# A block of 48 unused floats ahead of the normed activations in SBUF

## The reference

```
x = x + concat([y_a, y_b]) @ ev_w_out            # after h @ ev_w_in
x = x + conv_glu_ffn(rmsnorm(x), w_up, ..., w_down)
qkv = rmsnorm(x) @ od_w_qkv ;  x = x + y @ od_w_out
h = rms_norm(x) * (1 + scale) + shift            # second block
x = x + g * ((silu(h @ w_gate) * (h @ w_up)) @ w_down)
```

## Time and profile before

| | |
|---|---|
| median of three runs | 1253.51 us (1252.48 to 1256.44) |
| profiled execution: span | 1253.0 us |
| TensorE matmul busy | 1230.9 us, 98% of the span, 9987 matmuls |
| TensorE weight load busy | 1147.4 us, 92% |
| VectorE busy | 933.6 us, 75% |
| ScalarE busy | 703.9 us, 56% |
| TensorE on the chain that ended last | 97% of the span |
| granted TensorE clock | 0.999 of full |
| read from HBM | 261.17 MB, 209 GB/s |

### The profile page before, as it was taken

One profiled execution on the slowest core, in us unless ns is written; L12 is line 12 of the kernel. 1 busy time (PEld: TensorE's weight loads), 2 busy tenths in 40 slices (PEclk: granted clock), 3 DMA queues, 4 the chain that ended last, 5 costly groups with the idle time before them and its releaser, 6 DMA issues.

```text
span 1253.0 us, 23639 instructions
## 1 busy us (share of the span) xinstructions
PE 1230.9 (98%) x9987; PEld 1147.4 (92%) x9987; DVE 933.6 (75%) x1260; ACT 703.9 (56%) x1032; POOL 20.1 (2%) x31
## 2 busy tenths in 40 slices
PE   6999999999999999999999999999999999999998
PEld 6999889999999879999988998999998998999997
DVE  5888369888758777999987566899976666677453
ACT  6843477555555767666657556634445554643432
POOL 0002000000000000000000000000000000000000
PEclk9999999999999999999999999999999999999999
DMA  9450277776567256689653534899965356675540
GB/s 322 168 201 4 69 247 246 250 238 229 193 220 257 105 170 234 217 291 319 249 201 119 194 130 148 290 360 351 343 234 202 136 204 200 236 250 188 202 169 34
DMA packets 163683, 263.78 MB, mean 211 GB/s; under 512 B 5677, under 2 KB 98041, under 8 KB 163578
## 3 DMA queue, kind: packets, MB, share of 16 engines
q1 hardware_dynamic: 160586, 259.54, 60.3%
q10 hardware_dynamic: 2992, 2.72, 0.7%
HBM read 261.17 MB, written 1.05 MB: 209 GB/s over the span
## 4 chain that ended last, share of the span: by engine, by line
PE 97%; DVE 1%; ACT 1%; DMA 1%; issue 1%; SPq 0%; DVEq 0%; ACTq 0%
PE ps L1109 26%; PE ps L1080 17%; PE ps L1082 16%; PE ps L1081 16%; PE ps L847 2%; PE ps L848 2%; PE ps L849 2%; PE ps L1095 2%; PE ps L1097 2%; PE ps L1096 2%; PE ps L2397 2%; PE ps L827 1%; DMA ring<-in_ev_w_in_dram 1%; PE ps L2406 1%; PE ps L2597 1%
## 5 line engine op out<-in xcount | busy, mean ns | idle before, releaser
L623 DVE TENSOR_TENSOR wlo<-ring,whi 128x2048 fp32r<-128x2048 f32 x194 | 443.3, 2289 | 97.6 <-ACT whi L617 97.6
L1080 PE MATMUL ps<-ghi,whi 128*128 128x256 f32 x1600 | 449.0, 281 | 0.0
L1081 PE MATMUL ps<-glo,whi 128*128 128x256 f32 x1600 | 446.8, 279 | 0.0
L1082 PE MATMUL ps<-ghi,wlo 128*128 128x256 f32 x1600 | 446.5, 279 | 0.0
L617 ACT ACTIVATE whi<-ring 128x2048 fp32r<-128x2048 f32 x194 | 370.4, 1913 | 96.7 <-PE ps L1109 69.7
L1080 PEld LDWEIGHTS ps<-ghi,whi 128*128 128x128 f32 x1600 | 300.4, 188 | 2.0 <-DVE wlo L623 0.6
L1081 PEld LDWEIGHTS ps<-glo,whi 128*128 128x128 f32 x1600 | 299.7, 187 | 0.8
L1082 PEld LDWEIGHTS ps<-ghi,wlo 128*128 128x128 f32 x1600 | 300.4, 188 | 0.0
L1109 PE MATMUL ps<-whi,yhi 128*128 128x512 f32 x480 | 159.7, 396 | 0.7 <-DVE ylo L1996 0.7
L1109 PE MATMUL ps<-wlo,yhi 128*128 128x512 f32 x480 | 156.7, 390 | 0.0
L1109 PE MATMUL ps<-whi,ylo 128*128 128x512 f32 x480 | 156.6, 390 | 0.0
(11 more groups left out here) (314 smaller groups left out, 1575.0 us busy)
## 6 DMA issues: line engine op xcount, KB each, us to landing
arena<-in_w_ada_dram SPq DMA_DIRECT2D x48, 1024.0 KB, 6.0
ring<-in_ff_w_up_dram SPq DMA_DIRECT2D x44, 1024.0 KB, 7.6
ring<-in_w_gate_up_dram SPq DMA_DIRECT2D x44, 1024.0 KB, 7.5
ring<-in_ff_w_down_dram SPq DMA_DIRECT2D x10, 2048.0 KB, 7.9
ring<-in_w_down_dram SPq DMA_DIRECT2D x10, 2048.0 KB, 7.8
ring<-in_od_w_qkv_dram SPq DMA_DIRECT2D x6, 2048.0 KB, 8.6
ring<-in_w_qkv_dram SPq DMA_DIRECT2D x6, 2048.0 KB, 7.9
ring<-in_w_in_dram SPq DMA_DIRECT2D x6, 2048.0 KB, 8.1
```

The costliest lines, as they stand in the source:

```text
L623: e.tensor_tensor(shaped(WLO[i % NB], k), v, shaped(WHI[i % NB], k).bitcast(F32), ALU.subtract).then_inc(S["w_lo"], 1)
L1080: e.matmul(o, wh, h[0][:, k, :], start=k == 0, stop=False)
L1081: e.matmul(o, wh, h[1][:, k, :], start=False, stop=False)
L1082: x = e.matmul(o, wl, h[0][:, k, :], start=False, stop=k == NK - 1)
```

## The change

One line is added behind the declaration of `adahi` and `adalo`. It declares a block of 48 floats (192 bytes per partition) which nothing reads or writes:

```diff
         AHI, ALO = (sb(f"ada{i}", 512, F32R)[:, :] for i in ("hi", "lo"))
+        sb("gap_h", 48)
         MIX, PRE, SOLVE = ExitStack(), ExitStack(), ExitStack()
         RW = part(MIX, "mix", 32 * 256)
         HT0 = [c3(part(PRE, f"h{i}", NK * T, F32R)[:, :], NK) for i in ("hi", "lo")]
```

## The result

The changed kernel takes 1270.13 us in the median (1269.39 to 1270.59), the kernel before 1254.88 us in the same comparison. The ratio is 1.0129, 95% interval 1.0117 to 1.0141. The forecast was no change, so it was wrong. The profiled execution has a span of 1268.7 us, 15.7 more than before.

A forecast was written before the change was run, and what follows sets the result against it. TensorE, busy 1230.9 of 1253.0 us, was taken as the bound, the change acting only through matmul pace. All terms were 0 us, so the forecast was the median, 1253.5 us, range 1230 to 1261, no change at 0.52.

The forecast's parts named there:

- The four readings: Four observations from the profile, claiming that a tile's start doesn't decide between the paces of 113.3 and 117.7 ns.
- Reading 1: `pe_tile`, moving input at 960, stationary at 128 or 640: the same addresses give both paces, 113.3 and 117.7 ns.
- Reading 2: `pe_rows`, weights moving from 128, activations stationary from 960 or 448: the same two paces as `pe_tile`, 113.3 and 117.7 ns.
- Reading 3: Line 1109, both inputs already placed as after the change: 226.9 ns for 512 columns, so nothing below 113.3 ns gained.
- Reading 4: Weight loads on lines 1080, 1109 and 1096: 188 or 189 ns whether read from 128 or from 960 or 448.
- rows 4, 5 and 7: Profile timeline stretches of `pe_tile` (4, 5) and `pe_rows` (7), at 113.3 and 117.7 ns; cited for 0 us pace change.
- rows 9: Profile rows of weight loads, 188 or 189 ns at all offsets shown; cited for 0 on the 1248 matmuls with stationary activations.
- The upper bound: Most the tile matmuls could lose: 1680 on `pe_rows`, `pe_first` and `hhi` by 4.4 ns, 7.4 us.
- quick stretches turning slow: Rival: stretches at 113.3 ns (quick) go to 117.7 (slow), 3.7 to 7.4 us more, 1257 to 1261 us; chance 0.09.
- the collision: Rival: load and moving input, at the same offset, collide; 6480 matmuls by 4.4 ns, 28.5 us, 1262 to 1282 us; chance 0.09.
- The tiles turning quick: Rival: slow tile matmuls go to 113.3 ns, 21.1 us less; nearly all, 1230 to 1235 us, 0.15; part, 1236 to 1249, 0.13.
- The rule: The skill's step of N / 2.4 + 2.5 ns, 109.2 for 256 columns; reaching it would save 44 us, 1209 us; chance 0.02.

The follow-up runs named there:

- the sweeps: Separate kernels of matmul streams alone, weights at 128 or 960, sixteen activation starts 64 bytes apart: at distance 0 120.0 ns, at 64 and 192 113.3 or 117.8.

## Why the prediction was wrong

**What bounds the kernel** held: TensorE's pace is all of the change, and the scratch tiles behind `glo` cost nothing when they alone moved (1254.39 us against 1253.51 in the same comparison).

**The four readings** were right as rows and wrong as an argument. *Reading 1*: the same addresses give both paces. True, and it shows that a start doesn't fix the pace; it doesn't show that another start can't bring other paces. *Reading 2*: swapping the inputs changes nothing. By the sweeps the distances of the two kinds are 64 and 192, mirror images, and both have the pair 113.3 and 117.8. The swap that I took for a test of the offset was a test of its sign. *Reading 3* was true as written: line 1109, at distance 0, has 113.4 ns for each 256 columns, so both inputs at 128 "buy nothing below 113.3 ns". But it was the only row with both inputs at 128, and I let it stand for the short matmul. For 512 columns 0 is a good distance (227 against 232 at 128), for 256 columns it settles at the slowest pace seen (120.0). What the long matmul shows doesn't hold for the short one. *Reading 4*: loads take 188 ns at all offsets. It had no row of a 256-column matmul at distance 0, where they take 192.

**The step that failed** is in the sum: the pace of the 5232 tile matmuls was put at 0 ns "because rows 4, 5 and 7 are the case itself", and that of the 1248 with stationary activations at 0 by rows 9. None of these rows shows a matmul of 256 columns at distance 0; theirs are at 64 and 192. The runs showed in its place +2.3 ns for `pe_tile` (117.6 to 119.9), +5.1 for `pe_rows` and +3.6 for `pe_first`, 16.4 us together. The upper bound, 7.4 us, was for quick stretches turning slow, and so for two paces only. That there might be a third stood among the signs, and not in the bound.

**The rivals.** Of them the collision, at 0.09, came nearest: both inputs begin at the same offset, the loads get longer (192 ns), and 1270.13 us is in its range. Its price of 4.4 ns for each of 6480 was too high, since the new pace lies only 2.2 ns above the slow one: 16.3 us in place of 28.5. Its mechanism, a ns of pace for each ns of load, isn't shown: the loads of `pe_tile` grew by about 4 ns and its pace by 2.3, those of `pe_rows` by 3 and its pace by 5.1, and in the sweeps there is 120.0 ns with loads of 188 too (distance 96, and distance 0 behind matmuls of 512 columns with the weights at 960). Its argument against itself, the 188 ns of line 1109, was reading 4 again. The tiles turning quick was real as well, but at another distance than the change's.

**What decides** was named as what ran just before. That is half of it. The distance sets which paces there are, and what ran ahead has a part in which of them a stretch takes. The runs show both halves; by which resource of the chip two inputs at the same place modulo 256 get in each other's way, they don't. The Trainium skill ("TensorE: Matmul & The Clock Gate", "Step-by-step: what each phase is for") says that loading the next weights doesn't steal read bandwidth from the running matmul. Here load and matmul are not independent: `pe_tile` behind matmuls of 512 columns goes from 117.8 to 120.0 ns by a change that touches only starts in SBUF, and with them the distance between what is loaded and what moves. Whether read bandwidth is what they share, no run shows. Open, too, is how the phase at the start of a stretch picks the pace: behind the same eight transposes both paces occur in one kernel, as shown above, and nothing was run on that.

**The rule.** The prediction set N / 2.4 + 2.5 ns beside its rows. That section of the Trainium skill ("TensorE: Matmul & The Clock Gate", "Back-to-back issue gap") gives it for an isolated matmul, and says that in a stream of loads and matmuls both set the spacing; so the 109.2 ns were no rule for this stream. No stretch of any run settled below 113.3 ns for 256 columns.

## What to carry to other kernels

Where TensorE is the bound, look at the distance from start to start of its matmuls, and ask of the places in SBUF how far the moving input's start is from the stationary one's, modulo 256 bytes. Making both alike, which looks tidy, was the worst of the choices tried in the whole kernel; an unused block of 32 floats in place of 48 turned 1.3% lost into 0.4% won. And when the trace has no row of the case that a change creates, rows of like cases bound it only as far as the likeness is known: a mirror image or a longer matmul is not a test.

## What the runs showed of the hardware that was not expected

- A stream of float32 matmuls of 256 columns has discrete settled paces: 113.3, 116.7, 117.8, 120.0 ns, and some mixed ones between 117.3 and 118.7. It keeps one for as long as nothing comes in between: in the kernel before, 455 matmuls from 983.86 us on at 117.8.
- The pattern over the distance has a period of 256 bytes: 1270.13 and 1269.09 us with the activations at 128 and 384, and four repeats in each sweep.
- For the slowest pace it's the distance and not the place: 1270.13 us with both at 128, 1272.0 with both at 960, where the 512 columns are at distance 64 and add 1.5 ns each to the mean.
- A stream's pace depends on the distance of the stream ahead: nine of 14 stretches of `pe_tile` at 113.3 ns behind matmuls of 512 columns at distance 64, none of 14 at distance 0.
- Loads of 192 ns go with distance 0 alone in the sweep with the weights at 128. With the weights at 960, and behind matmuls of 512 columns, the pace at distance 0 was 120.0 with loads of 188 to 189 ns: the load's duration is a sign and not the measure.
